# The modulation product with its operands exchanged: weights stationary, four condition columns moving

## The reference

```python
cond_x = jax.nn.silu(c)
cond_c = jax.nn.silu(c_ctx)
for layer in range(DEPTH):          # DEPTH = 2
    mx = jnp.split((cond_x @ mod_w[layer] + mod_b[layer])[:, None, :], N_MOD, axis=-1)
    mc = jnp.split(cond_c @ mod_w[layer] + mod_b[layer], N_MOD, axis=-1)
    x = x + 0.5 * mx[2] * swiglu(modulate(rms_norm(x, norm_g[layer, 0]), mx[0], mx[1]), ...)
```

## Time and profile before

| | |
|---|---|
| median of 3 runs | 3116.46 us (3116.16 to 3118.27) |
| span of the profiled execution | 3115.2 us; its time with what lies around the span is not listed apart from the runs |
| PE busy | 2893.5 us, 93% |
| PEld busy | 2520.8 us, 81% |
| DVE busy | 1721.5 us, 55% |
| ACT busy | 1232.1 us, 40% |
| mean granted clock of TensorE | 0.954 |

### The profile page before, as it was taken

The page is one execution under the profiler, slowest core; times in us unless marked ns, Lnnn a source line. Parts: engine busy times, 40 slices in busy tenths (PEclk is TensorE's granted clock), DMA queues, the critical chain, the costliest instruction groups (busy, mean ns, idle before and its releaser), DMA issues.

```text
span 3115.2 us, 45778 instructions
## 1 busy us (share of the span) xinstructions
PE 2893.5 (93%) x17416; PEld 2520.8 (81%) x17416; DVE 1721.5 (55%) x2403; ACT 1232.1 (40%) x1488; POOL 0.2 (0%) x4
## 2 busy tenths in 40 slices
PE   7899899988998999699998898999989999889897
PEld 6888899987888999588886666888868888677897
DVE  6687667566866665624335645433353333566655
ACT  3364555443545554522323243323232232335443
POOL 0000000000000000000000000000000000000000
PEclk8999999999989999799999999999999999989998
DMA  7544467765444678224233201233232432320463
GB/s 222 157 151 153 154 210 232 220 174 149 156 143 155 211 231 232 75 70 123 74 95 87 81 1 54 75 98 111 76 86 82 115 94 79 103 68 23 135 189 101
DMA packets 584942, 393.06 MB, mean 126 GB/s; under 512 B 43670, under 2 KB 579124, under 8 KB 584628
## 3 DMA queue, kind: packets, MB, share of 16 engines
q1 hardware_dynamic: 584756, 390.57, 42.4%
HBM read 389.49 MB, written 1.05 MB: 125 GB/s over the span
## 4 chain that ended last, share of the span: by engine, by line
PE 83%; DVE 11%; ACT 4%; issue 2%; DMA 0%; SPq 0%; DVEq 0%; ACTq 0%
PE bank L1857 83%; DVE w_lo L1151 4%; ACT w_hi L837 2%; DVE t L1166 1%; DVE xs L1166 1%; DVE t L1159 1%; DVE rings L1166 1%; ACT t L841 0%; DVE acc L1159 0%; DVE h_lo L1166 0%; DMA raw<-in_w_in 0%; DVE score L1487 0%; DVE qk L1159 0%; DVE t L1163 0%; ACT gates L841 0%
## 5 line engine op out<-in xcount | busy, mean ns | idle before, releaser
L1151 DVE TENSOR_TENSOR w_lo<-raw,w_hi 128x2048 fp32r<-128x2048 f32 (+3 forms) x410 | 853.9, 2083 | 397.1 <-ACT w_hi L837 395.2
L837 ACT CAST w_hi<-raw 128x2048 fp32r<-128x2048 f32 (+3 forms) x410 | 711.8, 1737 | 691.6 <-PE bank L1857 673.2
L1857 PE MATMUL bank<-h_hi,w_hi 128*128 128x512 f32 (+1 forms) x1560 | 573.2, 367 | 51.0 <-DVE h_lo L1166 41.0
L1857 PE MATMUL bank<-h_hi,w_lo 128*128 128x512 f32 (+1 forms) x1560 | 569.1, 365 | 0.0
L1857 PE MATMUL bank<-h_lo,w_hi 128*128 128x512 f32 (+1 forms) x1560 | 568.1, 364 | 0.0
L1857 PE MATMUL bank<-x_hi,w_hi 128*128 128x256 f32 x1344 | 385.1, 287 | 20.1 <-DVE x_lo L1166 13.0
L1857 PEld LDWEIGHTS bank<-h_hi,w_hi 128*128 128x128 f32 x1560 | 297.3, 191 | 105.4 <-issue 47.8
L1857 PE MATMUL bank<-x_hi,w_lo 128*128 128x256 f32 x1344 | 378.9, 282 | 0.0
L1857 PE MATMUL bank<-x_lo,w_hi 128*128 128x256 f32 x1344 | 378.6, 282 | 0.0
L1857 PEld LDWEIGHTS bank<-h_hi,w_lo 128*128 128x128 f32 x1560 | 296.6, 190 | 49.8
L1857 PEld LDWEIGHTS bank<-h_lo,w_hi 128*128 128x128 f32 x1560 | 297.3, 191 | 47.8
(11 more groups left out here) (282 smaller groups left out, 4332.0 us busy)
## 6 DMA issues: line engine op xcount, KB each, us to landing
raw<-in_ffn_w_in SPq DMA_DIRECT2D x176, 512.0 KB
raw<-in_mod_w SPq DMA_DIRECT2D x72, 1024.0 KB
raw<-in_ffn_w_out SPq DMA_DIRECT2D x64, 704.0 KB
raw<-in_w_in SPq DMA_DIRECT2D x40, 1024.0 KB
raw<-in_w_ff_in SPq DMA_DIRECT2D x32, 1024.0 KB
raw<-in_w_ff_out SPq DMA_DIRECT2D x32, 1024.0 KB
raw<-in_w_out SPq DMA_DIRECT2D x8, 1024.0 KB
raw<-in_w_ple_gate SPq DMA_DIRECT2D x8, 1024.0 KB
```

What stands on the lines that cost most here:

```text
L837: act.copy(w_hi[s][:, w], raw[s][:, w]).then_inc(hi_made, c.did(hi_made))
L1151: dve.tensor_tensor(w_lo[s][:, w], raw[s][:, w], w_hi[s][:, w].bitcast(F32), ALU.subtract).then_inc(lo_made, c.did(lo_made))
L1857: ins = pe.transpose(o, l, r) if transpose else pe.matmul(o, l, r, start=start, stop=stop)
```

## The change

The modulation product exchanges its operands. The 128 x 128 tile of `w_hi` or `w_lo` is stationary, and the four condition columns of the inner tile move. The result comes out in columns: per output tile t, 4 columns (two conditions, high and low). For each of the 2 output tiles there are 8 inner tiles and 2 parts, so 32 matmuls in place of 16, each with 4 moving columns in place of 256. The turning matmuls, DVE's copy to `mod_rows`, the wait `rows_ready` and the constant `fold` go. DVE adds high part and bias, and then the low part, right behind each product: two small operations in place of a small one and a copy. `last_columns` and the turn behind the layer norm go as well.

```diff
-        cond_st = fixed("cond_st", [P, 4 * KT + P - 4], F32R)
+        cond_st = fixed("cond_st", [P, 4 * KT], F32R)
...
                     b = d_bank()
-                    if j:
-                        mod_columns(b, j - 1)
-                    copy(mod_rows[0:4, :], b[0:4, 0:256]).then_inc(d_free, c.did(d_free))
+                    mod_columns(b, j)
 
                 def mod_columns(b, j):
 
+                    out = mods[:, i, 4 * j:4 * j + 4].rearrange("p (t c) -> p t c", c=2)
+                    parts = b[:, 0:8].rearrange("p (t z c) -> p z t c", t=2, z=2)
                     dve.wait_ge(c.last, c.own())
-                    signal = d_free if j == MODS - 1 else v_step
-                    tt(mods[:, i, 4 * j:4 * j + 4].rearrange("p (t c) -> p t c", c=2),
-                       b[:, 256:260].rearrange("p (t c) -> p t c", c=2),
-                       cols_mod[:, i, 2 * j:2 * j + 2].unsqueeze(2).to_broadcast([P, 2, 2]), ALU.add).then_inc(signal, c.did(signal))
+                    tt(out, parts[:, 0], cols_mod[:, i, 2 * j:2 * j + 2].unsqueeze(2).to_broadcast([P, 2, 2]), ALU.add).then_inc(v_step, c.did(v_step))
+                    dve.wait_ge(c.last, c.own())
+                    tt(out, parts[:, 1], out, ALU.add).then_inc(d_free, c.did(d_free))
...
-                layer_norm(2, 3, last_columns)
+                layer_norm(2, 3)
...
                     if m % 2 == 0:
                         return
-                    if m > 1:
-                        rows_ready()
                     w = parts(chunk(), KT, 256)
                     pe.wait_ge(rd.free, rd.awaited())
                     b = rd.claim()
-                    if m > 1:
-                        mod_turn(b)
-
-                    for k in range(KT):
-                        for z in range(2):
-                            mm(b[:, 0:256], cond_st[:, 4 * k:4 * k + P], w[z][:, k, :], k == 0 and z == 0, k == KT - 1 and z == 1,
-                               d_full if k == KT - 1 and z == 1 else None)
-                    rows_at[0] = rd.used
+                    for t in range(2):
+                        for k in range(KT):
+                            for z in range(2):
+                                last = k == KT - 1 and z == 1
+                                mm(b[:, 4 * t:4 * t + 4], w[z][:, k, P * t:P * t + P], cond_st[:, 4 * k:4 * k + 4],
+                                   k == 0 and z == 0, last, d_full if t and last else None)
                     owed[0] = True
...
                 flush()
                 layer_norm_sums()
-                rows_ready()
-                pe.wait_ge(rd.free, rd.awaited())
-                mod_turn(rd.claim(), d_full)
```

More of the change, by code:

```diff
@@ L318, in constants @@
     out["rot"] = r
-    out["fold"] = np.tile(np.eye(2, dtype=f), (P // 2, 1))
     out["neg_tri"] = np.where(p >= k, -1, 0).astype(f)
@@ L339, in constants @@
     return out
-FIXED_CONSTS = {"ident": P, "ones": P, "rot": P, "fold": 2}
+FIXED_CONSTS = {"ident": P, "ones": P, "rot": P}
 PHASE1_CONSTS = {"neg_tri": P, "neg_ones": P, "row_mask": S, "sb_mask": S, "idx_mask": S,
@@ L441 @@
             'chunk_used': 108,
-            'd_free': 90,
-            'd_full': 90,
+            'd_free': 89,
+            'd_full': 89,
             'exp_made': 22,
@@ L573, in build @@
         x_sum = at("x_sum", 88, [P, S])[:, :]
-        mod_rows = at("mod_rows", 93, [P, 256])
         sq1 = at("sq1", 80, [P, KT, S])
@@ L616, in const @@
             return t[:, a:a + n]
-        ident, ones, rot, fold = (const(cst, n) for n in ("ident", "ones", "rot", "fold"))
-        cond_cols = cond_st[:, 0:4 * KT].rearrange("p (k c) -> p c k", c=4)
+        ident, ones, rot = (const(cst, n) for n in ("ident", "ones", "rot"))
+        cond_cols = cond_st[:, :].rearrange("p (k c) -> p c k", c=4)
         neg_tri, neg_ones, row_mask, sb_mask, idx_mask = (
@@ L1207, in _ @@
             dve.wait_ge(c.last, c.own())
-            copy(cond_st[:, 4 * KT:], raw[0][:, 0:P - 4]).then_inc(v_step, c.did(v_step))
-            dve.wait_ge(c.last, c.own())
             c.credit(lo_made, SLOTS)
@@ L1284, in layer_norm @@
                 variance(t1[:, 0, 0:S], b, D, LN_EPS)
-                if meanwhile is not None:
-                    meanwhile()
                 refine(t1[:, 0, 0:S], t1[:, 1, 0:S], t2[:, 0, 0:S])
@@ L1560, in _ @@
                     m += 1
-                def last_columns():
-                    dve.wait_ge(d_full, c.next(d_full))
-                    b = d_bank()
-                    mod_columns(b, MODS - 1)
-                layer_norm(2, 3, last_columns)
+                layer_norm(2, 3)
                 dve.wait_ge(x_ready, c.next(x_ready, KT))
@@ L1961, in done @@
                     b = rd.claim()
-                    if m > 1:
-                        mod_turn(b)
-                    for k in range(KT):
-                        for z in range(2):
-                            mm(b[:, 0:256], cond_st[:, 4 * k:4 * k + P], w[z][:, k, :], k == 0 and z == 0, k == KT - 1 and z == 1,
-                               d_full if k == KT - 1 and z == 1 else None)
-                    rows_at[0] = rd.used
-                    owed[0] = True
-                def rows_ready():
-                    pe.wait_ge(d_free, c.value(d_free, rows_at[0] + 1))
-                    pe.sem_inc(apart, 1)
-                def mod_turn(b, give=None):
-                    for t in range(2):
-                        mm(b[:, 256 + 2 * t:258 + 2 * t], mod_rows[0:4, P * t:P * t + P], fold[0:4, :], True, True,
-                           give if t else None)
+                    for t in range(2):
[4 more added lines that the diff above has]
+                                   k == 0 and z == 0, last, d_full if t and last else None)
+                    owed[0] = True
                 def two_tiles(w, ring, xk, give, made=None, per=1):
```

5 lines of the change are left out of this document (2 added, 3 removed).

## The result

The change makes the kernel slower: 3328.78 us (median of 4 runs, 3322.02 to 3335.8) against 3116.31 us (4 runs, 3115.5 to 3118.27). The ratio is 1.0684, 95% interval 1.0663 to 1.0704. Forecast were 3270 us and a range of 3162 to 3315. The direction was right, and the time lies 14 us above the range. The profiled execution of after has a span of 3334.0 us, 218.8 more than the one of before. It was the slowest of after's four; between the medians lie 212.5 us.

What follows compares the result with a forecast made beforehand. PE was taken to bound the kernel, mostly at full clock. Loads +65, clock falls +103, attention slack -12 and a vanished wait -3 gave +153 us on 3116.5, so 3270 us, range 3162 to 3315.

Steps and rivals of the forecast that it cites:

- loads: Modulation products: 32 matmuls at 0.11 us each make 3.52 us against 2.63 before; +65 us in sum.
- clock falls outside the attention: Products outside the attention: few moving columns look like a pause, the clock falls at three in four, 1.9 us each.
- loads and clock in the attention: Attention's 10 products: half of 0.89 us loads plus 1.4 us clock per product hidden by PE's slack, -12 us.
- place of the arrays: Addresses in SBUF: the prediction has no term for their shift.
- The rival of fast loads: Modulation products: loads follow each other 0.06 us apart, a product takes 1.9 us, execution 3066 us; chance 0.07.
- the one of small moving operands: Modulation products: by the Trainium skill's table some 25 ns per matmul without its load, a product 0.8 us; no separate chance.
- The rival of falls at nearly every product: Modulation products: the clock falls at nearly every one, often for long; time above 3320 us; chance 0.06.
- What else moves: Smaller effects beside loads and clock: attention slack -12 us, vanished wait for DVE's rows -3 us, DVE, banks, transfers 0.
- the rival without falls: Modulation products: no new clock falls, as loads count as work or thin stretches don't matter; +54 us, 3171 us; chance 0.22.

Runs made afterwards that it cites:

- e1: The changed kernel with 128 moving columns per matmul of the modulation product in place of 4, same result: 3211.01 us.
- e9: The changed kernel with every array at its address of before (unused constant `fold` and old length of `cond_st` kept): 3304.02 us.
- e13: The changed kernel with 256 moving columns per product matmul and unused `fold` kept, arrays behind `cond_st` 512 bytes further than in before: 3186.14 us.
- e12: The kernel before without the turning matmuls and their wait in all products but the last of each layer, most modulation values wrong: 3080.4 us.
- e2: The changed kernel with 256 moving columns per matmul of the modulation product in place of 4: 3205.12 us.
- e14: As e13, but the 10 products per layer in and around the attention move 4 columns, the other 26 move 256: 3243.12 us.
- e4: The changed kernel with one of two output tiles per product left out, 16 loads in place of 32, half the modulation wrong: 3129.46 us.
- e6: The kernel before with 32 bytes of padding ahead of the temporaries and work area, nothing else: 3160.3 us.
- e7: The kernel before with 64 bytes of padding ahead of the temporaries and work area, nothing else: 3148.33 us.
- e8: The kernel before with the turn done by two transposing matmuls in place of two float32 products, DVE adding in two sums: 3108.69 us.

## Why the prediction was wrong where it was

Step by step, with the terms of the prediction at the left. The intervals run from the start of one product to that of the next, 51 outside the attention and 20 in and around it. The last rows are not to be added to the first, since the loads of the attention stand in both.

| term | forecast | measured |
|---|---|---|
| loads | +65 | e1: first block +61.6 with the clock of before (with -3 and what was hidden) |
| clock falls outside the attention | 51 x 1.43 = 73 | after: 123.3 - 51 x 0.85 = 80; e9: 110.2 - 51 x 0.96 = 61 |
| loads and clock in the attention | 20 x (0.89 + 1.43) - 12 = 34 | after 65, e9 71 |
| place of the arrays | 0 | second block +30 |

**Right: the loads.** 0.11 us for each of 32, 3.48 us measured for 3.52 forecast, read from the loads of the two float32 matmuls of the turn. The rival of fast loads would have had 1.9 us, and the one of small moving operands 0.8. At an interval without a fall the next product starts 0.96 us later in e9 (0.88 and a longer second step of the main chunk behind it, 0.21 us, as the timeline above shows) and 0.85 in after, whose 96 main matmuls between two products take 11.29 us where they take 11.39 in e9.

**Right: the mechanism of the clock, its rate and the price of a fall.** e1 against after shows it, and e13 against e9 at harmless places: the same loads with 128 or 256 columns bring no more low clock than before has (99, 51 and 99 us). In after 37 of 51 intervals outside the attention have more time at 0.50 than before, 0.73 where three in four were forecast. Most have one of three lengths: 14.78 us without a fall (from 1232.06), 16.33 with one of 3.4 us (from 533.57), 17.93 with one of 6.8 us (from 1197.80), so a fall costs 1.55 or 3.15; 1.5 and 3.0 were forecast from two falls in the trace of before. The 80 us for 73 are of one execution, and e9's gave 61. The rival of falls at nearly every product named a time above 3320, and the time came out there, but not by that way.

**Wrong: "In the attention stretch (10 products) PE has slack. I take half of the 0.89 + 1.4 us per product as hidden: -12 us."** Slack is there for what PE gains, as e12 shows, and hardly for what it loses (e1, e2, e13). Above all the step mis-sized the clock term: it took the falls of the feed-forward part, on average 3.2 us at low clock per product (0.75 falls of 4.25 us), for the attention too. There the 20 intervals have 123 us more at low clock in after and 137 in e9, over 6 us each. In e9 the excess is worth 137 x 0.45 = 61 us, an estimate (0.45 is 1.53 / 3.41, the loss per us of low clock outside). With 20 x 0.96 for the loads that is 80, of which 71 came out. So 9 of 80 us were hidden over 20 intervals, where the prediction had half of what ten products cost, 12 of 23. The clock's part is twice the forecast one, 61 us for 20 x 1.43 = 29. By e14 these falls come from the attention's own products. Why a low clock lasts longer there (up to 17.1 us at a time in after, 44.4 in e4) was not taken apart.

**Wrong: the list "What else moves" is not complete.** It prices banks, transfers and a cast, but the diff's lines on `fold` and on the length of `cond_st` got no term: the place of the arrays was put at nothing, without a reason. The place of the arrays moved by 544 bytes, and the second block lost 30.0 us. e9, which differs from after in that alone, has 28 us of them back and takes 24.8 us less in all. The new place served the first block a little better (0.85 against 0.96 us per interval without a fall, 8 us over 71), which fits the difference, though that is smaller than the spread of the single runs. With the places of before the change takes 3304 us in the median, inside the range given; of its five runs two lie above it, at 3319 and 3321. The attention's 31 us alone would also have brought 3329 into the range, so neither miss alone put the time outside.

Together: 153 forecast, + 31 (attention, 65 - 34), + 30 (place), + 7 (falls outside), which makes 221, and 218.8 were measured between the two spans.

**A slip in the rival without falls.** It takes off 8 us as hidden, with only 0.89 per product. Half of that for ten products, as the forecast itself reckons, is 4.5 us, so its time would be 3174 and not 3171.

**The rest held.** PE waits no more for `mod_rows` and none for `mods` has come in its place; DVE has 7.1 us less to do (the prediction had reckoned with some 14 at most); no run prices that by itself. The tile `cond_st` in after: who waited for its products.

```profile
who waited for it (us, times):
  ACT w_hi L835: 192.7, 58
  DVE mods L1157: 10.0, 11
  DVE cond_st L1157: 0.3, 1
```

PE is not in the list, where it waited 2.9 us for `mod_rows` in before, and for the sums into `mods` it waits in neither kernel. ACT's 192.7 us are its wait for a slot to come free; in before it waited 203.7 us in the same way behind `mod_rows`.

## What to carry to other kernels

A matmul's price was here the longer of two times, that of its moving columns and that of the load of its stationary tile: with a new tile each, 0.11 us from start to start for 4 or 128 moving columns, 0.12 for 256, and 0.23 for 512. Before exchanging operands, count the loads on either side and read their pace from the one place in the trace where nothing hides them. A product that is bound by loads can also cost the clock while PE's busy share says 94%, so read the granted clock behind stretches with few moving columns, and in each kind of stretch by itself. And when a change shortens an array, hold the addresses of the others fixed in a second version: here the place alone was worth 1%.

## What the runs showed of the hardware that was not expected

- The pace of fp32r matmuls depends on where the moving operand lies in SBUF. With 512 moving columns it is 229.0 or 232.4 to 233.4 ns from start to start; with 256 it is 117.4 ns in before, 119.9 and 119.4 in e6 and e7, but 117.0 in after. Before + 64 bytes for the work area alone: +1.07%; + 64 bytes for all arrays: no change.
- The granted clock falls behind a stretch in which PE and PEld are busy for 3.42 of 3.42 us. With the same loads, the time at 0.50 in the first block was 391 us for 4 moving columns, 351 for 64, 99 for 128 and 82 for 256 (99 in before).
- Once low, it can stay so for 44.4 us with PE busy for 42.3 of them (e4), while in after and e9 every fall outside the attention ends after 3.4 or 6.8 us.
- Behind the turn the product's second matmul came 0.22 us after the first, with its two float32 matmuls (before) as with two transposing ones (e8); without the turn it came after 0.12 (e12).
